# Latent pages turned by block transfers and VectorE instead of TensorE, in a one-core decoder step

## The reference, cut to what matters

```python
def step(carry, phys):                       # for each page, all 8 sequences
    c_blk = cache_ckv[layer, phys]           # (8, 128, 256) latents of a page
    kp_blk = cache_kpe[layer, phys]          # (8, 128, 32) rotary keys
    kn_blk, v_blk = _decompress(c_blk, w_ukv, g_kn)      # keys 8 x 64, RMS-normed per head
    return _merge(carry, _attn_partial(qn, qp, kn_blk, kp_blk, v_blk, None)), None
```

## Time and profile before

| | us |
|---|---|
| median of 3 runs | 1372.71 (1370.44 to 1373.48) |
| the profiled execution | 1373.91 |
| its span | 1372.0 |
| PE busy | 1301.0, 95% |
| DVE busy | 707.8, 52% |
| ACT busy | 459.9, 34% |
| POOL busy | 150.8, 11% |
| DMA engines, share of their time | q1 18.1%, q10 1.2% |

### The profile page before, as it was taken

How to read it: one execution, slowest core, us unless ns; L and a number is a source line. 1 busy time by engine, 2 the same in 40 slices (tenths; PEclk the granted TensorE clock), 3 DMA queues, 4 the chain that set the end, 5 groups by cost and what they waited for, 6 DMA issues and landing times. The chain is left out here.

```text
span 1372.0 us, 26075 instructions
## 1 busy us (share of the span) xinstructions
PE 1301.0 (95%) x9543; PEld 750.1 (55%) x9543; DVE 707.8 (52%) x1749; ACT 459.9 (34%) x1108; POOL 150.8 (11%) x182
## 2 busy tenths in 40 slices
PE   5999999699999999999989999999999999989898
PEld 3545677556666666555445445666544444445343
DVE  3001436644665656555737876667666666520321
ACT  3001343233343433332434433434344444310220
POOL 0000314400020201114402230000000000000000
PEclk9999999789999999999999999999999999998999
DMA  5422121101111111131141113221334221101000
GB/s 206 155 74 54 32 62 32 52 19 37 37 37 37 37 37 37 37 71 36 40 129 41 40 39 113 97 90 43 86 112 116 68 69 53 49 0 35 16 16 35
DMA packets 82995, 81.49 MB, mean 59 GB/s; under 512 B 18946, under 2 KB 76611, under 8 KB 82868
## 3 DMA queue, kind: packets, MB, share of 16 engines
q1 hardware_dynamic: 80452, 73.87, 18.1%
q10 hardware_dynamic: 2416, 5.96, 1.2%
HBM read 75.72 MB, written 4.07 MB: 58 GB/s over the span
## 5 line engine op out<-in xcount | busy, mean ns | idle before, releaser
L500 PE MATMUL PS<-wk,c_T 128*128 128x512 f32 x1024 | 500.8, 612 | 0.0
L627 DVE TENSOR_REDUCE ssq<-sq__69 128x8 f32<-128x512 f32 x256 | 175.4, 685 | 221.1 <-ACT sq__69 L554 218.7
L500 PEld LDWEIGHTS PS<-wk,c_T 128*128 128x128 f32 x1024 | 176.3, 192 | 163.0 <-issue 145.7
L554 ACT ACTIVATE sq__69<-PS 128x512 f32<-128x512 f32 x256 | 152.8, 597 | 320.5 <-PE PS L500 320.2
L455 PE MATMUL PS<-cst,c_ring 128*128 128x128 f32 x512 | 83.0, 287 | 24.7 <-DVE c_ring L663 10.1
L1470 PE MATMUL PS<-xnT,w_ring 128*128 128x276 f32 x416 | 104.7, 409 | 0.0
L455 PEld LDWEIGHTS PS<-cst,c_ring 128*128 128x128 f32 x512 | 60.4, 147 | 69.7 <-issue 45.0
L1304 PE MATMUL PS<-w_ring,xnT 128*128 128x424 f32 x256 | 95.3, 530 | 2.1 <-DMA w_ring<-in_w_in 2.1
L1470 PEld LDWEIGHTS PS<-xnT,w_ring 128*128 128x128 f32 x416 | 79.9, 195 | 21.9 <-issue 4.1
L1304 PEld LDWEIGHTS PS<-w_ring,xnT 128*128 128x128 f32 x256 | 48.5, 193 | 46.8 <-issue 44.3
L2655 PE MATMUL PS<-w_g,nT 128*128 128x512 f32 x128 | 56.0, 594 | 0.0
(11 more groups left out here) (534 smaller groups left out, 1873.3 us busy)
## 6 DMA issues: line engine op xcount, KB each, us to landing
c_ring<-in_cache_ckv SPq DMA_DIRECT2D x256, 128.0 KB, 2.8
w_ring<-in_w_in SPq DMA_DIRECT2D x4, 1696.0 KB, 14.4
w_ring<-in_w_in SPq DMA_DIRECT2D x9, 512.0 KB, 5.0
r_ring<-in_cache_kpe SPq DMA_DIRECT2D x256, 16.0 KB, 1.8
w_o<-in_w_out SPq DMA_DIRECT2D x8, 512.0 KB, 3.7
w_g<-in_w_ple_gate SPq DMA_DIRECT2D x8, 512.0 KB, 3.6
xn<-in_x_prompt SPq DMA_DIRECT2D x4, 512.0 KB, 7.0
w_ring<-in_w_in SPq DMA_DIRECT2D x2, 1024.0 KB, 5.8
```

Source lines behind the costliest of these rows:

```text
L500: mm = pe.matmul(PS[:, NORM[v % 2], :], c_T[:, u % 2, k, t * P:(t + 1) * P], wk[:, k], start=(k == 0), stop=(k == 1))
L554: nc.scalar.activation(sq_[:, v % 2, :], PS[:, NORM[v % 2], :], ACT.Square).then_inc(no_sb, 1)
L627: dve.tensor_reduce(ssq[:, u % 2, t * H:(t + 1) * H], sq_[:, v % 2, :].rearrange("p (h c) -> p h c", h=H), AX.X, ALU.add).then_inc(red_sb, 1)
```

## The change

It has one large part and several small ones.

1. The latents are no longer turned by PE. `latent_blocks` copies, inside the on-chip memory, 64 channels (one quarter of 256) of all 128 partitions of `c_ring` into 32 partitions of the new buffer `c_blocks`: four DMAs a step of 128 KB each, in pieces of 64 numbers (256 B), two issued by SP and two by ACT. DVE then turns 32x32 tiles (`STREAM_TRANSPOSE`, 256 columns in one instruction, four a step) straight into `c_T`. `c_blocks` and `c_T` have one place each instead of two for `c_T`; `c_ring` has 5 places, `r_ring` 3. The rows of `wk` are loaded in the order of channels that this gives.
2. `turn_r` is in slot 0, `dots` in slot 1. The copy of the dot products is on ACT (slot 3). The page numbers are loaded without range check.
3. ACT issues its two block DMAs behind `square(u, 1)`. DVE turns tile 0 of the next step behind `score` in slot 2, tiles 1 and 2 in slot 3, tile 3 in slot 0. SP issues its two when the last tile of the step before has been turned.
4. Chunks, samples' scan and latents are one block (`chunk_*`, `seqs_*`, `lat_*` are called one after the other), so two barriers are gone; the samples' scan has 24 slots, the tail one less.
5. The first quarter of `w_in` is loaded right behind tile 0, PE's transposes of a tile stand in the middle of a projection, `wk` is loaded by eight DMAs, and the preparation's steps stand ahead of the column group's copies instead of behind.
6. The causal mask is added by DVE, in PSUM, ahead of the maximum; the mask matmul is gone.

```diff
+        def latent_blocks(eng, u, groups_c):
+            eng.wait_ge(c_in[u % RING], 16 * GT * (u // RING + 1))
+            if u >= 1:
+                eng.wait_ge(ct_sb, u * GT)
+            for g in groups_c:
+                eng.dma_start(c_blocks[32 * g:32 * g + 32].rearrange("p x t c -> p (x t c)"),
+                              c_ring[:, slot_of[u], :, g * (KVL // 4):(g + 1) * (KVL // 4)]).then_inc(b_in, 16)
+
         def pages_sp():
             sp = nc.sync
-            for u in range(NSTEP):
+            latent_blocks(sp, 0, (0, 1))
+            for u in range(NSTEP + 2):
+                if 1 <= u - 2 < NSTEP:
+                    latent_blocks(sp, u - 2, (0, 1))
...
             def dots(u):
+                pe.wait_ge(ct_sb, u * GT + GT)
                 pe.wait_ge(tn_sb, u + 1)
...
             def norms(u, t):
                 v = u * GT + t
-                if t == 0:
-                    pe.wait_ge(k1_sb, u + 1)
+                pe.wait_ge(ct_sb, v + 1)
...
             for u, t in slots:
-                ahead = u + 1 < NSTEP
                 if t == 0:
-                    if ahead:
-                        turn_c(u + 1, 0)
+                    turn_r(u)
                     if u >= 2:
                         turn_weights(u - 2)
                 if t == 1:
-                    if ahead:
-                        turn_c(u + 1, 1)
+                    dots(u)
                     if u >= 2:
                         values(u - 2)
-                if t == 2:
-                    turn_r(u)
-                    if u >= 1:
-                        turn_scale(u - 1)
-                if t == 3:
-                    dots(u)
+                if t == 2 and u >= 1:
+                    turn_scale(u - 1)
                 norms(u, t)
                 yield
...
+            def turned_c(u, t):
+                dve.wait_ge(b_in, 16 * 4 * (u + 1))
+                if u >= 1:
+                    dve.wait_ge(rp_ps, u)
+                    dve.wait_ge(no_ps, (u - 1) * GT + t + 1)
+                dve.transpose(c_T[:].rearrange("p k (t a x) -> p t x k a", t=GT, x=GT)[:, t],
+                              c_blocks[:, :, t, :].rearrange("p x (k c) -> p x k c", k=2)).then_inc(ct_sb, 1)
...
@@ -2556,8 +2598,8 @@
-                    pe.matmul(bank(u % 2)[:, 0:w], qT[:, h, i * P:(i + 1) * P], k_T[:, h, 0:w], start=True, stop=False)
-                    pe.matmul(bank(u % 2)[:, w - P:w], ident, con("causal"), start=False, stop=True).then_inc(sc_ps, 1)
+                    pe.matmul(bank(u % 2)[:, 0:w], qT[:, h, i * P:(i + 1) * P], k_T[:, h, 0:w], start=True, stop=True
+                              ).then_inc(sc_ps, 1)
```

More of the change, by code:

```diff
@@ L673, in pages_dve @@
                     merge(u - 2)
-                if t == 2 and u >= 1:
-                    score(u - 1)
-                if t == 3:
-                    dotted(u)
+                if t == 2:
+                    if u >= 1:
+                        score(u - 1)
+                    if ahead:
+                        turned_c(u + 1, 0)
+                if t == 3 and ahead:
+                    turned_c(u + 1, 1)
+                    turned_c(u + 1, 2)
                 reduce(u, t)
@@ new lines, in chunk_pe @@
+                mm.then_inc(l_ps, 1)
+                for h in range(H):
+                    for ck in HALVES:
+                        mm = pe.matmul(eight(2, ck)[:, at_head(h), :], gram[ck, at_head(h), 2, :],
+                                       vn[ck, i, h * HN:(h + 1) * HN], start=True, stop=True)
+                mm.then_inc(w_ps, 1)
+                on_pe.go(2)
+                pe.wait_ge(low_sb, 3 * i + 1)
+                products(0, gram[:, :, 0], low[:, 0])
+                products(1, low[:, 0], gram[:, :, 0]).then_inc(y2_ps, 1)
@@ new lines, in chunk_pe @@
+                on_pe.go(1)
+                pe.wait_ge(u5_sb, i + 1)
+                pe.wait_ge(low_sb, 3 * i + 3)
+                turns(3, ua)
+                products(0, low[:, 2], ua).then_inc(t5_ps, 1)
+                on_pe.go(1)
+                pe.wait_ge(t5_sb, i + 1)
+                products(1, pa[:, 0], pa[:, 1]).then_inc(u6_ps, 1)
+                on_pe.go(1)
+                pe.wait_ge(u6_sb, i + 1)
+                for o in range(H):
+                    for ck in HALVES:
+                        mm = pe.matmul(bank(2 + o // 4)[ck, (o % 4) * P:(o % 4 + 1) * P], ub[ck, o, :], aw[ck, o, :, :],
+                                       start=True, stop=True)
@@ new lines, in chunk_pe @@
+                mm.then_inc(rt_ps, 1)
+                for h in range(H):
+                    o, j, hs = at_head(h), h // 2, slice(h * HN, (h + 1) * HN)
+                    for c, ck in enumerate(HALVES):
+                        dst = bank(2 + c)[hp(h), j * HN:(j + 1) * HN]
+                        pe.matmul(dst, bk[ck, 1, hs], vn[ck, i, hs], start=True, stop=False)
+                        mm = pe.matmul(dst, bk[ck, 0, hs], nw[ck, o, 1, :], start=False, stop=True)
+                mm.then_inc(h_ps, 1)
@@ new lines, in chunk_pe @@
+                on_pe.go(1)
+                pe.wait_ge(rt_sb, i + 1)
+                pe.wait_ge(s_clear, 1)
+                for h in range(H):
+                    mm = pe.matmul(bank(0)[hp(h), h // 2 * HN:(h // 2 + 1) * HN], gt[hp(h), 0, h // 2, :],
+                                   st[hp(h), 2 * i % 3, h // 2, :], start=True, stop=True)
+                mm.then_inc(s_ps, 1)
+                pe.wait_ge(hc_sb, i + 1)
+                for h in range(H):
+                    o, j, hs = at_head(h), h // 2, slice(h * HN, (h + 1) * HN)
+                    for ck in HALVES:
+                        dst = eight(2, ck)[:, o, :]
+                        pe.matmul(dst, gram[ck, o, 1, :], nw[ck, o, 1, :], start=True, stop=False)
+                        mm = pe.matmul(dst, gram[ck, o, 3, :], vn[ck, i, hs], start=False, stop=True)
```

1708 lines of the change are left out of this document (842 added, 866 removed).

## The result

| | before | after |
|---|---|---|
| median, us (4 runs each) | 1372.12 | 1486.68 (1471.07 to 1491.64) |
| ratio | | 1.082, 95% interval 1.073 to 1.090 |
| span of the profiled execution | 1372.0 | 1480.4 |
| mean granted clock of TensorE | 0.973 | 0.930 |

The kernel is 8% slower. 1318 us was predicted, with a range of 1283 to 1366; sign and size are wrong. The rival that ended on the other side, C (the blocks land late), is what happened, and at a higher price than its 1398 us. One of the four runs of small_parts further down, 1390.28 us at a granted clock of 0.93 where the others have 0.98, was a slow one and is left out of its numbers.

A forecast was written before the change was run, and what follows sets the result against it. PE was taken as the bound in all five stages, DVE second. Terms 3 - 16 - 3 - 4 - 15 - 10 - 7 - 3 = -55 from 1373.9 gave 1318.9, median forecast 1318 us, range 1283 to 1366.

The forecast's parts named there:

- C (the blocks land late): DVE waits ahead of tile 0 for late blocks, ending slower than before: 1398 us at a 5.5 us landing; chance 0.11.
- the landing in Part 1: Tail: block copies replacing PE's transposes land 2.8 us after issue, 2.2 to 3.5 allowed.
- The square-to-tile piece: Tail: from ACT's square of slot 1 at 1059.05 to the block's arrival at 1062.4.
- the prediction's chain: Tail step through norms, square, block copies, DVE's tiles and dots: 10.0 us, 0.15 more than now; +3 us in all.
- Rows 3: Profile rows showing PE's granted clock at 0.60 to 0.80 around pauses; costed at 1.7 us behind each barrier.
- In the attention the term: Attention: step falls from 16.1 to 14.3 us with transposes and mask off PE, -15 us, bounds -21 to -5.
- The mask: Attention: mask matmul leaves PE, 0.38 us a unit, four a step, -1.5 us a step.
- The pauses: Two barriers, 4.6 and 5.8 us of PE standing plus slow clock behind each: -5.5 and -4.5 us.
- The tile: DVE's turn of one 256-column tile, four a step, takes 0.42 us.
- rival B: DVE's tile takes 0.7 us instead of 0.42, adding 41 us across the stages: 1359 us; chance 0.15.
- the start and the preparation: PE waits less for first weights, -3 us, and starts page work at about 266 instead of 269.6, -7 us.
- the value of the transposes for PE: Each step loses 0.99 us of PE work; in the chunks 17 steps, less 1, give -16 us.

The follow-up runs named there:

- small_parts: Changed kernel with the old page work put back: PE turns the latents, the start, fused blocks and DVE mask stay; 1351.67 us, 0.984 of the kernel before.
- early_blocks: Changed kernel with ACT's two block transfers issued behind square of slot 0 instead of slot 1; 1357.42 us, 0.988 of the kernel before.
- best: Changed kernel with ACT's blocks behind square of slot 0, dense tiles reordered by ACT, and the causal mask on PE; 1333.13 us, 0.970 of before.
- filler: Changed kernel with sixteen discarded identity transposes on PE ahead of its wait for c_T, each tail step; 1457.98 us.
- quarter_loads: Changed kernel with latent page loads from step 5 on bringing a quarter of the bytes, for time only; 1398.6 us.
- wide_pieces: Changed kernel with the same block transfer bytes in pieces of 1 KB instead of 256 B, wrong latents turned; 1438.13 us.
- pair_ring: early_blocks with the blocks in three places of two tiles each, copied in 64 KB transfers, eight a step; 1350.72 us.
- filler_attn: filler with its extra transposes from step 33 on instead of 41, so in the attention too; 1461.81 us.
- small_maskpe: small_parts with the causal mask back on PE as a second matmul, none on DVE; 1356.28 us.
- early_dense: early_blocks with tiles written densely and the order of positions put right by two strided ACT operations; 1343.61 us, 0.978 of the kernel before.
- dense_tiles: Changed kernel with tiles written in rows of 128 neighbouring numbers, positions left in another order; 1466.7 us in a single run.

## Why the prediction was wrong

Microseconds against the kernel before, between the same steps of the profiled executions. The stretch from step 18 to 32 is two fused blocks, samples' scan and latents.

| stretch | predicted | after | early_blocks | small_parts | best |
|---|---|---|---|---|---|
| up to `norms` of step 0 | -10 | -12.2 | -11.8 | -15.2 | -11.4 |
| steps 0 to 17 (chunks) | -16 | -2.5 | -14.9 | -1.4 | -17.0 |
| steps 18 to 32 | -17 | +6.0 | +0.4 | -2.1 | -7.1 |
| steps 33 to 40 (attention) | -15 | +30.8 | +3.7 | -2.5 | -4.9 |
| steps 41 to 62 (tail) | +3 | +85.8 | +9.9 | +0.7 | +0.6 |
| the rest | 0 | +0.5 | -2.1 | -1.6 | -0.5 |
| sum | -55 | +108.4 | -14.8 | -22.1 | -40.3 |

**The step that failed first is the landing in Part 1.** "The nearest row in bytes is the page load, 128 KB and 2.8 us" was a row taken in a kernel whose DMA engines were 28% busy. Two things were missing. Even without a page load beside it a copy took 3.3 us: that is near the 3.5 which the prediction's own price of small pieces gave (2.8 and 0.7) and which it kept for its upper bound only. And ACT's second copy, for which tile 0 waits, is issued beside four page loads, with a DMA share of 0.50 in the tail, and landed in 4.8 us in the step shown and in 5.5 us in the median of the tail. An issue took 0.66 us where 0.53 was added. The square-to-tile piece is 5.9 us in that step instead of 3.35: 2.5 us by 22 steps are 55 us, and the tail in filler, without the clock's part, is at +60. quarter_loads and wide_pieces show that traffic and pieces both have a share in it, early_blocks that most of it is off the path if the copy is issued one slot earlier. The rest of the prediction's chain held: 3.1 and 3.4 us of it came out as drawn. That most tail steps of early_blocks take 9.8 us, close to the 10.0 of the prediction, is chance: they follow another ring, the one without PE shown above, and pair_ring, which has no such ring, needs 10.0 too.

**A cost that had no term is the clock.** Rows 3 showed that PE is slow behind a pause, and the sum used it for the two barriers only. A wait of 3 us in every step was not asked for it. It cost 20 to 26 us in the tail, shown by filler.

**In the attention the term had the wrong bound.** 14.3 us a step were expected from DVE's busy time; 20 were measured. DVE was busy for 105.7 of 158.6 us, so it isn't the load but the order: what waits in DVE's queue holds back the maxima of the prompt attention, and these hold back ACT, for which PE stood 27.5 us. early_blocks took 27 us off the stage. filler_attn speaks against the clock as the cause, within the scatter of that stage (157 to 168 us in the kernels with the late block and all page loads), but does not exclude a share of it. quarter_loads, with the block late but less so, needed 135.5 us. **The mask** was sized from the busy time of its matmul, 0.38 us a unit. small_maskpe against small_parts is 3.8 us of the attention for 32 units, 0.12 each: so most of the busy time in that row lies over that of other matmuls. And its other end, DVE, was costed as covered; in early_blocks it was 8.7 us on the path. An edit of -12 us was one of +9 where the tiles are on DVE, and -4 without them.

**The pauses.** The barriers' waits are gone, as predicted, but most of the time came back elsewhere: small_parts has -2.1 us over the two stages where -10 was put down. Steps 18 to 23, in which both barriers lay, took 10.3 us less than before (105.9 against 116.2), and steps 24 to 32 took 8.2 us more (150.6 against 142.4). Its rows of PE's waits:

```profile
PE PS L2253 <- DMA wukv<-in_w_ukv: 6.9, 1, 6.9
...
PE PS L2253 <- DVE nat L2353: 2.9, 3, 1.4
```

A wait for `wukv` has taken the place of the second barrier's 5.8 us. SP issued that load of 1 MB at 677.15 us, behind stores of the samples' scan, and it landed 8.2 us later, when PE went on; an earlier issue was not tried. In the changed kernel the two stages took 8 us more than in small_parts (+6.0 against -2.1), most of which early_blocks took off (+0.4).

**The tile** was mis-sized by the write: 0.628 against 0.42 us, rival B's condition. Beside early blocks the dense tile gave 14 us net of ACT's longer exponentials (early_dense), less than B's 41; in the changed kernel the single run of dense_tiles is too few to say, since it lies 4 us below the fastest of a kernel whose runs are 20 us apart.

**What was right:** the start and the preparation (-12.2 against -10; PE's first `norms` at 262.1 us); the value of the transposes for PE, 0.99 us a step: the chunks gave -14.9 in early_blocks and -17.0 in best where -16 was put down, as soon as the block was in time. In the changed kernel itself even the chunks lost most of it. **Rival C** had place and queue right. Its price for the tail, 22 us for each microsecond above 2.8, fits too: in filler, where the clock is out of it, the copy that counts landed after 5.1 us (median of the tail), which gives +3 and 51, and +60 was measured. Its break-even of 4.8 us wasn't tested; with the median of 4.4 us the formula would still have given a faster kernel. Its chance of 0.11, of which half was to lie above 1373 (0.06, not the 0.08 that was given for slower), rested on a DMA share of 0.28 that the change itself was to nearly double, and its price left out the clock and DVE's queue in the attention.

## What to carry to other kernels

When a new transfer stands on the path, take its landing as a range from the traffic that will be there after the change, and ask first how many microseconds earlier it could be issued: here one statement, one slot up, was worth 129 us, while page loads of a quarter of the bytes were worth 88 and pieces four times as long 49. Look at the copy that lands last, not at the median of all. Count for each new wait what is queued behind it on its engine, and give PE's clock a term where PE will stand in every step: such a stall can cost more than its own length. And don't price a matmul by its busy time where matmuls follow one another: take the distance between starts.

## What the runs showed of the hardware

- Sixteen extra transposes in a wait made the 352 matmuls of `norms` in the tail faster by 26.8 us: work whose result is thrown away can pay where PE stands in every step. In the attention the same did not pay (filler_attn).
- A transpose of 32x32 tiles in fp32 by VectorE, 128x256 numbers in all, takes 0.63 us when it writes one number in four and 0.43 us when it writes densely. The two strided operations on ACT that put the order right took 265 ns (the rotary keys, as before) and 512 ns instead of 390 (the exponentials).
- Copies of 128 KB inside the on-chip memory, in pieces of 256 B, landed 3.3 us after the issue with no page load beside them (54 of SP's) and 4.4 after it where page loads were mostly under way (ACT's), 3.6 with a quarter of the page loads' bytes; of two issued one behind the other beside page loads the second took 5.5 us in the tail, the first 4.0. A copy of half the size landed in 2.3 to 2.7 (medians).
